# A hybrid decoder step on one core: the scan's chunk load in two parts, fills on GpSimd, and the hand-over from the running sequences' pass to the merge

## The reference

```python
h = rmsnorm(x, norm_w)
z, xbc, dt, qkv, a, b, gate, mg_ssm, mg_gdn = split_cols(h @ w_in, IN_SIZES)
xbc = silu(causal_dwconv(xbc, ...) + ssm_conv_b);  qkv = silu(causal_dwconv(qkv, ...))
# chunked scans; the states of the prompt and of every running sequence are outputs too
y_ssm, hs = ssd_segment(xs, Bm, Cm, dt, A, hs)          # 32 heads
y_gdn, S = gdn_segment(q, k, v, g, beta, S)             # 8 heads, a triangular solve in each chunk
y_ssm = rmsnorm(y_ssm * silu(z)) @ w_ssm_out
y_gdn = (rmsnorm(y_gdn) * silu(gate)) @ w_gdn_out
merged = sigmoid(mg_ssm) * y_ssm + sigmoid(mg_gdn) * y_gdn
x = x + merged @ w_o
gt, up = split_cols(rmsnorm(x) @ w_up, (D_FF, D_FF))
y = rmsnorm(x + (silu(causal_dwconv(gt, ...) + conv_b) * up) @ w_down)
```

## Time and profile before

| | us |
|---|---|
| median of 3 runs (lowest, highest) | 3218.35 (3214.18, 3218.46) |
| the profiled execution | 3209.63 |
| its span, first to last instruction | 3207.8 |
| TensorE busy (share of the span) | 2930.1 (91%) |
| VectorE, ScalarE, GpSimd busy | 1521.4, 1035.7, 391.9 |

### The profile page before, as it was taken

The page is one execution under the profiler, slowest core; times in us unless marked ns, Lnnn a source line. Parts: engine busy times, 40 slices in busy tenths (PEclk is TensorE's granted clock), DMA queues, the critical chain, the costliest instruction groups (busy, mean ns, idle before and its releaser), DMA issues. The chain is left out here.

```text
span 3207.8 us, 50873 instructions
## 1 busy us (share of the span) xinstructions
PE 2930.1 (91%) x18908; PEld 2785.1 (87%) x18908; DVE 1521.4 (47%) x2288; ACT 1035.7 (32%) x2130; POOL 391.9 (12%) x540
## 2 busy tenths in 40 slices
PE   3799999999999979999999776999889999997998
PEld 2799999999999968777878536999879999997998
DVE  5355555531101158887888564554453332323443
ACT  3222222221111135545545252332331211113332
POOL 2000000000000022422332210000110000000100
PEclk7899999999999989999999777999989999998999
DMA  2222222232233222353244447644422112125443
GB/s 79 72 94 94 94 94 88 87 106 94 90 108 119 87 71 66 74 114 72 65 109 65 154 148 284 209 156 152 167 75 80 60 70 95 60 85 184 167 145 108
DMA packets 238744, 348.05 MB, mean 109 GB/s; under 512 B 154520, under 2 KB 173288, under 8 KB 238368
## 3 DMA queue, kind: packets, MB, share of 16 engines
q1 hardware_dynamic: 233264, 325.20, 32.1%
q0 software_dynamic: 5360, 21.29, 1.8%
HBM read 253.24 MB, written 93.22 MB: 108 GB/s over the span
## 5 line engine op out<-in xcount | busy, mean ns | idle before, releaser
L534 PE MATMUL pps<-h_hi,pwh 128*128 128x352 f32 (+1 forms) x2112 | 689.2, 326 | 16.0 <-DVE pwl L599 16.0
L534 PE MATMUL pps<-h_hi,pwl 128*128 128x352 f32 (+1 forms) x2112 | 686.4, 325 | 0.0
L534 PE MATMUL pps<-h_lo,pwh 128*128 128x352 f32 (+1 forms) x2112 | 684.6, 324 | 0.0
L534 PEld LDWEIGHTS pps<-h_hi,pwh 128*128 128x128 f32 x2112 | 397.2, 188 | 16.4 <-issue 16.4
L534 PEld LDWEIGHTS pps<-h_lo,pwh 128*128 128x128 f32 x2112 | 397.8, 188 | 0.0
L534 PEld LDWEIGHTS pps<-h_hi,pwl 128*128 128x128 f32 x2112 | 397.5, 188 | 0.0
L2326 PE MATMUL u_ps<-f_hi,up_wh 128*128 128x352 f32 (+1 forms) x1056 | 346.0, 328 | 8.5 <-DVE up_wl L2318 8.5
L599 DVE TENSOR_TENSOR pwl<-pw,pwh 128x1024 fp32r<-128x1024 f32 x88 | 107.8, 1226 | 505.4 <-ACT pwh L547 498.2
L2326 PE MATMUL u_ps<-f_hi,up_wl 128*128 128x352 f32 (+1 forms) x1056 | 345.0, 327 | 0.0
L2326 PE MATMUL u_ps<-f_lo,up_wh 128*128 128x352 f32 (+1 forms) x1056 | 345.0, 327 | 0.0
L2326 PE MATMUL merge_ps<-merge_yh,merge_wh 128*128 128x352 f32 (+1 forms) x576 | 190.2, 330 | 34.1 <-DVE merge_yl L2472 26.2
(11 more groups left out here) (455 smaller groups left out, 5164.6 us busy)
## 6 DMA issues: line engine op xcount, KB each, us to landing
projected<-pO SPq DMA_DIRECT2D x88, 536.0 KB, 3.0
pw<-in_w_in SPq DMA_DIRECT2D x88, 512.0 KB, 4.0
merge_w<-in_w_out SPq DMA_DIRECT2D x72, 512.0 KB, 3.3
down_w<-in_w_down SPq DMA_DIRECT2D x48, 704.0 KB, 4.0
up_w<-in_w_up SPq DMA_DIRECT2D x44, 512.0 KB, 4.5
chunk<-projected SPq DMA_DIRECT2D x5, 3744.0 KB, 16.8
scan_chunk<-projected SPq DMA_DIRECT2D x5, 3744.0 KB, 16.6
wo_w<-in_w_o SPq DMA_DIRECT2D x24, 512.0 KB, 3.3
```

Of the source, the lines that this page charges most:

```text
L534: ins = pe.matmul(ps[:, 3 * u + n, 0:cn], l[u][:, k, :], r[:, k, c0:c0 + cn], start=(k == 0 and a == 0), stop=(k == KD - 1 and a == 2))
```

## The change

1. In the scan, a chunk's transfer is split: `load` fetches the 48 tiles as soon as the chunk two before has issued its last products with q (`m_QS`), ahead of `store`; `load_gates` fetches the 24 gate tiles after the store has landed. TensorE waits for the gates only at its first use of them.
2. At the scan's start GpSimd fills `D`, `S` and `h`; the fill of `ss` is dropped, the copy of the selector comes first on VectorE, and ScalarE's `identities` stands after the first norms.
3. The buffer `chunk0` becomes the front of `place`, a buffer of 3 x 8 x 368 that also serves as merge's `raw`. The running pass loads merge's first activations into its third part (they are of prompt columns, stored by the scan), ahead of the last two stores of `ssm_new`. `run_kn` moves into it too.
4. The running pass no longer awaits the stores of `gdn_new`; merge's first writes of `m_hi` and `m_lo` do (`states_out`), since these lie over `run_S`. The phase that filled ones is gone (the first tile of ones stays). The tail's buffers change sides.
5. In merge and down each unit's activations are converted, and waited for, in two parts; in merge the third unit's remainder at a column turn stands after the sums; in down the first weight's split stands between the two parts, the table load of ScalarE behind them, and the other weights are requested when the first has landed.

The diff's core (helpers and unchanged arguments cut):

```diff
             def load(t, u):
...
-                sp.dma_start(cd[u][:, :, :], scratch[0:NSCAN, :, bass.ds(t * C, C)].rearrange(
+                sp.dma_start(cd[u][:, 0:XT + GT, :], scratch[0:XT + GT, :, bass.ds(t * C, C)].rearrange(
                     "m p n -> p m n")).then_inc(loaded.sems[u], 16)
+
+            def load_gates(t, u):
+                sp.dma_start(cd[u][:, XT + GT:, :], scratch[XT + GT:NSCAN, :, bass.ds(t * C, C)].rearrange(
+                    "m p n -> p m n")).then_inc(gates_in.sems[u], 16)
...
                 for u in range(2):
+                    sp.wait_ge(m_QS.sem, m_QS.at(2 * i + u))
+                    load(2 * i + u + 2, u)
                     store(2 * i + u, u)
                     sp.wait_ge(stored.sems[u], stored.at(i))
-                    load(2 * i + u + 2, u)
+                    load_gates(2 * i + u + 2, u)
...
+            for tile in (D[:, :, :, :, :], S[:, :, :, :], h[:, :, :]):
+                pool.memset(tile, 0.0).then_inc(zeroed.sem, 1)
...
             for j in range(2 * G):
+                if j == 2 * G - 2:
+                    sp.wait_ge(m_KQ, 2)
+                    sp.wait_ge(m_inter, G)
+                    sp.wait_ge(p_kw, 1)
+                    sp.dma_start(place[:, 2, :, :], mixed[0:KD, :, 0:NCOL[0][1]].rearrange("k p n -> p k n")).then_inc(next_in, 16)
...
-            sp.wait_ge(state_out, 16 * HALF)
+            sp.wait_ge(next_in, 16)
...
+                for half, ks in enumerate(halves):
+                    dve.wait_ge(y_hi.sem, y_hi.at(nu * n + unit, half + 1))
+                    part = slice(k + ks[0], k + ks[-1] + 1)
+                    dve.tensor_tensor(yl[:, part, 0:cn], source_of(unit)[:, ks[0]:ks[-1] + 1, 0:cn],
+                                      yh[:, part, 0:cn].bitcast(F32), ALU.subtract).then_inc(y_lo.sem, 1)
...
+                if isinstance(m, int) and m == KD - 1 and n < 2:
+                    convert(n + 1, nu - 1)
                 dve.wait_ge(hi_done[u].sem, hi_done[u].at(rnd))
+                if n == 0:
+                    dve.wait_ge(states_out, STATES_OUT)
...
             for s in range(2 * nu):
+                if s == 1:
+                    sp.wait_ge(ring.loaded.sems[0], ring.loaded.at(0))
                 ring.load(sp, s, s, s)
```

More of the change, by code:

```diff
@@ L1108, in _ @@
             q_sizes(0)
-            pe.wait_ge(zeroed.sem, zeroed.at(0))
+            pe.wait_ge(sel_copied.sem, sel_copied.at(0))
             chunks(pe, body)
@@ L2319, in split_lo, with product @@
                                           ALU.subtract).then_inc(self.lo_done.sem, 1)
-    def product(self, pe, u, out, hi, lo, first=True, last=True):
+    def product(self, pe, u, out, hi, lo, first=True, last=True, ks=None):
         ku = self.raw.shape[2]
-        for k in range(ku):
+        for k in ks or range(ku):
             for a, (l, r) in enumerate(((self.hi[u], hi), (self.hi[u], lo), (self.lo[u], hi))):
@@ L2448, in start @@
                     convert(n, unit)
+                    if unit == 0:
+                        for s in range(2):
+                            ring.split_hi(act, s, s, s, 1)
             def body(n, m, u, rnd, s0):
@@ L2477, in start @@
                     convert(n, unit)
+                    if unit == 0:
+                        for s in range(2):
+                            ring.split_lo(dve, s, s, s)
             def body(n, m, u, rnd, s0):
@@ L3085, in masks_of_shapes @@
     return np.concatenate([np.asarray(m[n], np.float32) for n, _, _ in MASKS], 1)
-def ones_phase(nc, ones):
-    with phase(nc) as ctx:
-        block = ctx.enter_context(nc.Block())
-        @block.vector
-        def _(dve):
-            dve.memset(ones[:, :], 1.0)
 def program(nc, d):
```

169 lines of the change are left out of this document (95 added, 74 removed).

## The result

| | before | after |
|---|---|---|
| median of the runs | 3216.26 us (3210.22 to 3218.46, 4 runs) | 3162.99 us (3161.58 to 3172.0, 4 runs) |
| ratio | | 0.9849, 95% interval 0.9834 to 0.9864 |
| span of the profiled execution | 3207.8 us | 3170.2 us |

The change makes the kernel faster by 1.5%: 48.6 us off 3218 by the ratio, with the interval from 44 to 53, where 45.3 was forecast. The profiled execution of after is the longest of its four runs (3172.0), and its span is only 37.6 us shorter. So the same kernel was profiled once more (called "again" here, span 3159.6). The table cuts the spans at instructions that both kernels have; the last column is what the prediction's terms put there.

A forecast was written before the change was run, and what follows sets the result against it. TensorE, busy 91% of the span, was taken as the bound, so time could be won almost only at its waits or lower clock. Six terms sum to 45.3 us: 3218.35 - 45.3 = 3173 us, range 3162 to 3190, chance 0.60.

The forecast's parts named there:

- The scan's start: Scan's start: fills on GpSimd and identities behind the norms bring TensorE's sums of squares 5.3 us sooner; 3.7 without cover.
- The chunk load: Scan's eight steps: requesting keys earlier removes TensorE's waits for the chunk transfer, 10.1 us; ends 2 and 12.
- The running pass into merge: Merge's start: unawaited stores, early activations and half conversions bring the third unit 11.0 us sooner; ends 3 and 15.
- a sign of this step: Profile after should show merge's third unit 10 to 11 us sooner after the same start of the running pass.
- Merge's column turns: Merge's two turns: halves and the third remainder behind the sums cut TensorE's weight waits, 3.6 us; ends 2 and 7.
- a sign of a wrong forecast: Whole kernel: the forecast is wrong if TensorE's clock falls at places where it held before.
- Down's start: Down's first product: with half conversions the weight is the last link, 4.1 us sooner; ends 2 and 5.
- Down's column turns: Down's two turns: halves remove 7.2 us of waits and the clock holds, 4.0 more; 11.2 us, ends 6 and 13.
- (a): Merge's weights come late as GpSimd's loads take the larger share; term 3 shrinks to about 4, 3180 us; chance 0.14.
- (b): Scan has another bound: VectorE or ScalarE replaces the wait, term 2 gives 2, 3181 us; chance 0.10.
- (c): Half conversions do not reach TensorE; terms 4 to 6 give 10 instead of 18.9, 3182 us; chance 0.12.
- (d): Slower: state stores are starved and merge's first column block waits for them, some 52 us needed; chance 0.02.

The follow-up runs named there:

- one_request: Changed kernel with each scan chunk loaded by one request of 72 tiles behind the store of the chunk before; 3178.01 us, ratio 0.9905 to before.
- late_keys: Changed kernel with a chunk's 48 key tiles requested behind the store of the chunk before, gates in their own request; 3162.70 us, ratio 0.9851 to before.
- the six profiles: Profiles in which merge and what leads into it stand as changed; VectorE's last running-pass sum to the residual phase's first product 318.9 to 321.5 us, mean 320.0.
- down_whole: Changed kernel with each unit's activations in down converted in one part again; 3174.70 us, ratio 0.9886 to before.

## Why the prediction was right, step by step

The forecast of 3173 and its range from 3162 to 3190 held the median, 3162.99, at the range's lower edge. The difference of 8.7 us between profile and median that the forecast carried over from three runs of before is a good part of the 10 us between them: before's medians in the later rounds were 3207 to 3210, and for an execution like the profiled one the forecast was 3164.3, where again's profiled execution took 3161.41.

Against the profile of again (48.2 us shorter than that of before) the sum of 45.3 was near in part by luck: from the scan to the running pass 18.2 us came instead of 15.4 and in up's stretch 7.1 instead of 4.1, while merge up to the residual phase gave 10.2 instead of 14.6. The terms stand as follows.

1. **The scan's start, 5.3.** Right: 5.6 at the sums of squares, 4.7 to 6.2 when undone. Both covers held: the identities stand behind the norms without making the first step longer, and GpSimd's fills are done at 1147.2, before anyone asks.
2. **The chunk load, 10.1: too small, and for a reason that was half wrong.** The waits were the path, but the steps gave 13.1 us, and 14.7 when the request was made whole again. Of the 14.7, 11.7 are TensorE's waits for the chunk; the rest stands behind them, in part at the lower clock, as in the row of one_request above, where eight transposes take 1.90 us instead of 1.04. I had put that in as the upper end of 12 and then not taken it. The reason I gave, the request 48 us ahead of the use, is not what helps: late_keys asks late and loses nothing. What helps is that the keys are told of apart from the gates.
3. **The running pass into merge, 11.0: too large.** The start was right: the first product 12.6 us sooner (11.6 predicted), the weight landing 7.6 us after its request, between the two values I had worked out (6.2 and 9.6; worked again from its own figures, with half the rate from 1934 on, the later one is 9.3). The step that failed is the bytes and their rate up to the third unit. I had 6.95 MB at 407 GB/s, 17.1 us; from the first load until the third activations were in, 20.0 us later, after moved

```profile
DMA packets 2068, 7.35 MB, mean 367 GB/s; under 512 B 147, under 2 KB 435, under 8 KB 2066
```

   More bytes, because SyncE asks for the next weights at 1925.98, as soon as a ring place is free, and GpSimd for the next block's activations at 1921.21 (3.29 MB moved in its queue where I had 3.01). And a lower rate: 406 GB/s up to 1918.6, and then

```profile
1918.60:1921.10 2.50, 0.00 (x0) 0.00 (x0) 2.32 (x2) 0.31 (x1) 0.00 (x0) 0.50 0.99 221
1921.10:1935.87 14.77, 8.46 (x38) 8.19 (x39) 5.74 (x4) 4.87 (x4) 1.44 (x2) 0.70 1.02 385
```

   In the first of these stretches no packet of GpSimd's queue moved yet. SyncE's queue (q1) alone kept the transfer engines busy:

```profile
q1 hardware_dynamic: 148, 0.55, 98.8%
```

   So the dip to 221 is not GpSimd's share; what makes it, no run here shows.

   The first load came 2.25 us after VectorE's last sum, 1.0 later than I had put it. So 7.7 us at the third unit instead of 11.0, and below the 10 to 11 that I had named as a sign of this step.
4. **Merge's column turns, 3.6.** Right in the waits: 6.9 us of them became 3.4. In the time from the third unit to the residual phase (293.2 before) only 1.6 of it shows by the mean of the six profiles (291.6): a wait of 4 us at the third unit, followed by products at half clock, stood in no term. The unit's products took 6.2 us by that mean where they took 4.1 before, at 1.00. That is the fall of the clock, at a place where it held before, that I had named as a sign of a wrong forecast; it cost 2.1 us.
5. **Down's start, 4.1.** Right: 4.2 from the first load to the first product, of which 2.95 are the halves and 1.3 the table load, when the halves are undone first. The prediction moved ScalarE's first half back by the table load at no cost; it had left out VectorE's first half remainder (2.46 us) behind it, so a part of this term came from the table load's new place, which I had priced at nothing. The whole stretch from up's first product is 7.1 shorter; the other 3 us lie in up and its end, part of them at the lower clock, and belong to no edit that I can name.
6. **Down's column turns, 11.2.** Right: 11.4, and 10.5 when undone. The waits gave 5.8 instead of 7.2 (0.2 to 0.6 us are left three times a turn); the rest, 5.6, is more than the 4.0 that I had put down to the clock, so two misses offset each other. That the clock holds when the wait is gone was the uncertain half of this term, and the stretch at 1.00 that answers to the earlier trace rows shows it; in down_whole, with the wait back, the stretch is at 0.50 again.

Of the rivals, (a) was right in direction: up to the residual phase merge's start and turns gave 9.1 us by the mean of the six profiles instead of 14.6. But the first weight was late by the stores ahead of it in its own queue (3.5 us after its request where two of them stand behind it), and the third unit by all that the queues held. (b) and (c) fell: no other engine took the place of the scan's wait, and the halves reach TensorE. (d) had nothing for it: no engine was seen to wait for the state stores in merge, even where GpSimd issued two of them last.

## What to carry to other kernels

A transfer that only misses its use by a microsecond or two need not be asked for earlier: split the request where the first reader's part ends, so that this part has its own semaphore. Behind a phase that ends with large stores, count every request that goes out until TensorE's buffers are full, those that a freed ring place sets off too, at a rate measured over such a stretch (367 GB/s here) and not at that of the stores alone (407); while the transfers run at full rate, another order of the requests mostly moves the wait, unless what is put behind is wanted by nobody yet. Before a difference of some microseconds between two profiles is put down to an edit, look at the granted clock and the landing times in the stretches whose code is the same.

## What the runs showed of the hardware that I had not expected

- Two requests of 2.56 and 1.28 MB, 0.5 us apart on one queue, landed 12.5 and 16.8 us after the first one; one request of 3.83 MB landed after 16.7. These loads have rows of 416 bytes and move at 230 GB/s (3.83 MB in 16.7 us), against 385 GB/s in merge's start from 1921.1 on.
- One kernel's residual phase took 119.2 and 124.9 us in two executions. The granted clock was 0.94 and 0.91, up's first weight landed 3.4 and 6.4 us after its request, and the busy times of VectorE, ScalarE and GpSimd were equal within 0.15 us.
- Behind a wait of 1.85 to 1.95 us at merge's second turn the next 24 products ran at granted 0.69 in four of the six profiles (5.5 us) and at 1.00 in the other two (4.0 us).
- Loads behind state stores moved 367 GB/s over 20 us at merge's start, with 2.5 us at 221 before the second queue's first packet, where the state stores alone had moved 407.
- A wait of 3.6 us at down's turn was followed by products at granted 0.50, three waits of 0.2 to 0.3 us with 5 us of products between them were not (1.00 throughout).
